# Expert weights in unbroken halves: four neighbouring rows to a partition, in a two-layer MoE and hybrid-mixer kernel

## The chip, the core and the metric

The kernel runs on one NeuronCore of a Trainium2 chip. Its engines are TensorE (PE, matmuls and transposes), VectorE (DVE), ScalarE (ACT), GpSimd (POOL) and SyncE (SP, which here only issues transfers); 16 DMA engines move data between HBM and the on-chip memory. The metric is the device time of one execution in microseconds (us), the median of several runs.

## The reference

A sequence of 512 tokens with 1024 features goes through two blocks of two layers each. Only the feed-forward part of the first block's two layers is touched by the change: a mixture of 16 experts of width 256, of which each token uses two.

```python
def _moe(h, w_router, router_bias, w_gate, w_up, w_down):
    t = h.reshape(b * s, d)
    scores = jax.nn.sigmoid((t @ w_router).astype(jnp.float32))
...
    combine = jnp.sum(jax.nn.one_hot(idx, N_EXPERTS, dtype=jnp.float32) * gate[..., None], 1)
    hg = jnp.einsum('td,edf->tef', t, w_gate)
    hu = jnp.einsum('td,edf->tef', t, w_up)
    act = jax.nn.silu(hg) * hu * combine[..., None].astype(t.dtype)
    y = jnp.einsum('tef,efd->td', act, w_down)
```

Left out is the choice of the two best experts of the best group of four. `w_gate` and `w_up` are [16, 1024, 256] in a layer, `w_down` is [16, 256, 1024].

Everything is float32. The kernel reaches that precision with three products: each matrix is split into a rounded high part and the remainder, its low part, and high x high, high x low and low x high are added.

## The kernel before

**Stages.** The program is a row of stages, each ended by a barrier of all engines. The change touches two kinds, each of which runs twice, once a layer: `norm_to_hT` where it has a `Router` (normalises, transposes, computes the router's scores, and loads small tables), and right behind it `moe` (the expert stage). In the profile the expert stages run from about 584 to 930 us and from about 1512 to 1860 us.

**Blocks of tokens.** `moe` sorts the 1024 (token, expert) pairs into 23 blocks of 128 rows, each of one expert: blocks 0 to 15 are those of experts 0 to 15, and seven more take what overflows. GpSimd scatters the normalised rows to the HBM tensor `slots_x`. For each block, `x_rows(b)` loads 128 rows of 4 KB from there to `x_block`, a row to a partition. TensorE transposes them with eight instructions in `to_features` (to PSUM), ScalarE scales and shifts each of the eight results with a column of `pk` (`mod_pk`, two tables of 8 columns) into `x_exact`, VectorE splits that into high and low parts (`xT_hi`, `xT_lo`), and TensorE multiplies with the gate and up weights. ScalarE and VectorE form silu(gate) x up (`sg`, `act_t`), TensorE transposes it and multiplies with the down weights, VectorE scales the result (`y_block`), and ScalarE's queue stores it to `slots_y`.

**Units of weights.** A block needs three units of 1 MB: A and B, each with half of the expert's gate matrix and half of its up matrix, and C, its down matrix. `BlockUnits.order` is A0 B0 A1 B1 C0 A2 B2 C1 and so on; the SP queue issues their loads in that order, A and B as two transfers of 512 KB (gate, up), C as one of 1 MB, and x_rows(b + 2) behind each C. There are four raw buffers (two in `raw_sep`, two in `ring`), so a load waits until the unit four places before it has been split. ScalarE makes the high part of each unit (L2152, `split_high`), VectorE the low part of A and C (L2206, `split_low`), GpSimd the low part of B from block 2 on (L2059). The parts live in six places, whose names in the profile are `w_hi`/`w_lo`, `hT_hi`/`hT_lo` and `w_more_hi`/`w_more_lo`.

**Which rows a unit holds.** A matrix has 1024 rows of 1 KB, one to an input feature. Before the change, partition p owns the eight neighbouring rows 8p to 8p + 7 (8 KB). Unit A takes the first four of each partition (`ks = slice(0, 4)`), unit B the last four. So each transfer of 512 KB reads 128 pieces of 4 KB that start 8 KB apart: every second 4 KB of the expert's 1 MB. The features that go with slot k are k, 8 + k, 16 + k and so on, so the transposes in `to_features` read their input in steps of 8 elements (32 bytes), and `pk` is loaded with 8 neighbouring values to a partition. The down matrix of unit C is one unbroken megabyte.

**The lines that the steps below name.** L1136 and L1138 store the modulation columns to HBM and load them back as `mod_pk`; L2023 loads `x_block`; L2038 loads unit C, L2044 the two transfers of A or B; L2094 is the transposes, L2102 and L2105 the gate and up products, L2139 and L2143 the down products; L2159 is `x_exact`, L2152 the high parts, L2206 and L2059 the low parts, L2275 and L2276 the split of `x_exact`, L2301 the low part of the transposed activations (`aT_lo`), L2282 `y_block`.

Of the kernel before, what the change touches and what calls it, by code (L numbers as in the profile page):

```python
# [14 lines left out]
P = 128  # L15
S = 512
NT = S // P
D = 1024
KD = D // P
# [1091 lines left out]
class Router:  # L1111
# [16 lines left out]
    def load(self, sp):  # L1128
        k = self.k
# [5 lines left out]
        sp.dma_start(self.tri[:], k.K["causal"][:, 0, :]).then_inc(self.landed, 16)  # L1135
        sp.dma_start(cols.rearrange("(j p) -> p j", p=P), k.mod[:, 24:40], allow_slow_non_contiguous=True).then_inc(self.pk_landed, 16)  # L1136
        sp.wait_ge(self.pk_landed, 16)
        sp.dma_start(self.pk[:], cols.rearrange("(i p k) -> p i k", i=2, k=KD)).then_inc(self.pk_landed, 16)  # L1138
        sp.wait_ge(self.landed, 96)
        sp.wait_ge(self.pk_landed, 32)  # L1140

    def split(self, dve, link):
        V = self.k.nc.vector
# [820 lines left out]
def moe(k, l, hT, wg, wu, wd, grow, router):  # L1964
# [4 lines left out]
    with ExitStack() as c:  # L1969
# [47 lines left out]
        def _(sp):  # L2017
# [7 lines left out]
            for s, (kind, b) in enumerate(U.order):  # L2025
# [11 lines left out]
                if kind == "C":  # L2037
                    sp.dma_start(dst, wd[e].rearrange("e p f n -> p (e f n)")).then_inc(done, 32)  # L2038
                    if b + 2 < NB and b > 0:
                        x_rows(b + 2)  # L2040
                else:
                    ks = slice(0, 4) if kind == "A" else slice(4, 8)
                    for i, w in enumerate((wg, wu)):
                        sp.dma_start(dst[:, i * D:(i + 1) * D], w[e, :, ks, :].rearrange("e p k n -> p (e k n)")).then_inc(done, 16)  # L2044
                if s == EARLY + 1:
                    x_rows(2)

# [22 lines left out]
        def _(pe):  # L2070
# [17 lines left out]
            def to_features(b):  # L2088
                pe.wait_ge(x_landed[b % 2], 16 * (b // 2) + 16)
                if b >= 1:  # L2090
                    pe.wait_ge(ex_done, b)
                v = xb[:, b % 2, :].rearrange("p (f k) -> p k f", k=KD)
                for q in range(KD):
                    mm = pe.transpose(k.ps[:, 2 + q // 4, (q % 4) * P:(q % 4 + 1) * P], v[:, q, :], k.ident[:])  # L2094
                mm.then_inc(t_done, 1)

            def gate_up(b, kind, first, last):
# [11 lines left out]
            for b in range(NB + 1):  # L2109
                v = b - 1  # L2110
# [206 lines left out]
def first_layer(k, l, last_store):  # L2317
# [4 lines left out]
    with ExitStack() as c:  # L2322
# [31 lines left out]
        with ExitStack() as m:  # L2354
            hT = pair_of(nc, m, "hT", [P, KD, S])
            router = Router(k, m)
            norm_to_hT(k, hT, False, LN_EPS, k.mod[:, 32:40], k.mod[:, 24:32], affine=(A["ln1_g"][l], A["ln1_b"][l]), router=router)
            ex = lambda ap, kp: ap.rearrange("l e (p k) n -> l e p k n", k=kp)[l]
            moe(k, l, hT, ex(A["w_exp_gate"], KD), ex(A["w_exp_up"], KD), ex(A["w_exp_down"], 2), g2, router)
    norm_to_hT(k, None, False, LN_EPS, None, None, affine=(A["ln2_g"][l], A["ln2_b"][l]), store=last_store)  # L2360


# [1234 lines left out]
```

## Time and profile before

| | us |
|---|---|
| median of 3 runs | 3776.25 |
| lowest and highest of them | 3766.58, 3776.66 |
| the profiled execution, its own time | 3776.66 |
| its span (first to last instruction) | 3774.8 |

| engine | busy, us | share of the span |
|---|---|---|
| PE (matmul) | 3225.0 | 85% |
| PEld (weight load) | 2560.7 | 68% |
| DVE | 2407.0 | 64% |
| ACT | 1278.6 | 34% |
| POOL | 573.7 | 15% |

The two expert stages are about 345 us each, 18% of the span. These shares are means over stages with different limits; in the expert stages the engines and the transfers stand otherwise than in the rest, so what counts is read from stretches inside them. The profiled execution took 0.41 us more than the median, and its span is 1.9 us under its own time.

### The profile page before, as it was taken

Reading aid. Unit: us, or ns where it says so; the run is one execution under the profiler, and the core shown is the slowest. Engines: PE = TensorE matmul, PEld = TensorE weight load, DVE = VectorE, ACT = ScalarE, POOL = GpSimd, SP = SyncE. Lnnn points to the kernel's source line nnn. Section 1 sums busy time; section 2 is a strip of 40 time slices with the busy share of each in tenths; the row PEclk is TensorE's granted clock in tenths of the full one; section 3 lists DMA queues with packets and bytes.
Section 4 is the critical chain, followed back from the end, with each engine's and each line's share of the span. In section 5 each row is a group of like instructions: output and inputs, shape, how many; then the busy total and the mean of one; then the engine's idle time right before and its main releaser. Section 6 shows DMA issues by size and latency. Waiting matters only on the chain. (4 is left out here: it accounts for less than half of the span.)

```text
span 3774.8 us, 41000 instructions
## 1 busy us (share of the span) xinstructions
PE 3225.0 (85%) x14702; PEld 2560.7 (68%) x14702; DVE 2407.0 (64%) x3790; ACT 1278.6 (34%) x2024; POOL 573.7 (15%) x147
## 2 busy tenths in 40 slices
PE   4999977885699996788489799678999899889999
PEld 4767756664576685666367578566887688667887
DVE  6756676987676657699743746467775564565445
ACT  2323224674323323476322624232111322231111
POOL 0000002443000000234200000102444100004443
PEclk9999988998799998899789799788999899869999
DMA  7643525997554452799552033012443253102232
GB/s 276 221 165 115 193 96 203 338 341 243 196 175 162 149 171 83 260 339 336 212 188 99 9 110 120 27 56 92 142 144 112 86 176 110 73 23 90 89 100 78
DMA packets 290090, 584.97 MB, mean 155 GB/s; under 512 B 26233, under 2 KB 134193, under 8 KB 282732
## 3 DMA queue, kind: packets, MB, share of 16 engines
q1 hardware_dynamic: 277528, 538.91, 42.6%
q10 hardware_dynamic: 7764, 26.85, 1.8%
q0 software_dynamic: 4608, 16.78, 1.2%
q8 instruction: 108, 1.77, 0.2%
q14 instruction: 82, 0.67, 0.1%
HBM read 529.45 MB, written 79.76 MB: 161 GB/s over the span
## 5 line engine op out<-in xcount | busy, mean ns | idle before, releaser
L132 ACT CAST w_hi<-ring 128x2048 fp32r<-128x2048 f32 (+2 forms) x166 | 308.0, 1859 | 1205.6 <-PE ps L282 1032.1
L282 PE MATMUL ps<-hT_hi,w_hi 128*128 128x512 f32 (+1 forms) x1256 | 500.5, 399 | 22.7 <-DVEq L1108 9.2
L282 PE MATMUL ps<-hT_lo,w_hi 128*128 128x512 f32 (+1 forms) x1256 | 498.5, 397 | 0.0
L139 POOL TENSOR_TENSOR w_lo<-ring,w_hi 128x2048 fp32r<-128x2048 f32 x64 | 307.0, 4798 | 1035.1 <-ACTq L2763 649.6
L144 DVE TENSOR_TENSOR w_lo<-ring,w_hi 128x2048 fp32r<-128x2048 f32 (+3 forms) x112 | 245.4, 2195 | 238.4 <-ACT w_hi L132 238.1
L282 PE MATMUL ps<-hT_hi,w_lo 128*128 128x512 f32 (+1 forms) x1256 | 305.3, 395 | 8.4 <-DVE w_lo L144 8.4
L282 PEld LDWEIGHTS ps<-hT_hi,w_hi 128*128 128x128 f32 (+1 forms) x1256 | 238.5, 190 | 83.1 <-DVEq L1108 10.8
L282 PEld LDWEIGHTS ps<-hT_hi,w_lo 128*128 128x128 f32 (+1 forms) x1256 | 235.9, 188 | 65.4 <-DVE w_lo L144 10.1
L1047 DVE SCALAR_TENSOR_TENSOR piece_sums<-pieces,cond,piece_sums 128x512 f32<-128x512 f32 x294 | 220.8, 751 | 87.6 <-DMA pieces<-in_w_ada_dram 54.8
L282 PEld LDWEIGHTS ps<-hT_lo,w_hi 128*128 128x128 f32 (+1 forms) x1256 | 238.5, 190 | 55.6
L282 PE MATMUL ps<-w_hi,hT_hi 128*128 128x512 f32 (+1 forms) x672 | 260.0, 389 | 1.0 <-ACT w_hi L132 1.0
L282 PE MATMUL ps<-w_hi,hT_lo 128*128 128x512 f32 (+1 forms) x672 | 259.0, 387 | 0.0
L1322 PE MATMUL ps<-ident_sb,ring 128*128 128x128 f32 x160 | 37.9, 425 | 205.0 <-ACT ring L1285 150.0
L2053 POOL DMA_INDIRECT slots_x<-ring,rows_r x16 | 26.5, 1656 | 1207.3 <-DVE rows_r L2250 1203.1
L2159 ACT ACTIVATE x_exact<-ps,mod_pk 128x128 f32<-128x128 f32 x368 | 133.7, 468 | 161.1 <-PE ps L2094 161.1
L1322 PEld LDWEIGHTS ps<-ident_sb,ring 128*128 128x128 f32 x160 | 32.6, 229 | 210.0 <-ACT ring L1285 154.2
L282 PE MATMUL ps<-w_hi,hid_hi 128*128 128x512 f32 x448 | 174.4, 389 | 0.0
L282 PE MATMUL ps<-w_hi,hid_lo 128*128 128x512 f32 x448 | 174.4, 389 | 0.0
L2828 DVE TENSOR_TENSOR hid_exact<-hid_exact 128x512 f32<-128x512 f32 x64 | 162.0, 2531 | 4.0 <-DVE hid_exact L2825 0.6
L102 PE MATMUL ps<-ident_sb 128*128 128x128 f32 x796 | 115.4, 317 | 54.1 <-PEq L72 45.5
L282 PE MATMUL ps<-w_lo,hT_hi 128*128 128x512 f32 (+1 forms) x672 | 158.2, 387 | 0.0
L102 PEld LDWEIGHTS ps<-ident_sb 128*128 128x128 f32 x796 | 113.0, 232 | 57.8 <-issue 49.1
(588 smaller groups left out, 6760.5 us busy)
## 6 DMA issues: line engine op xcount, KB each, us to landing
ring<-in_mlp_w_dram SPq DMA_DIRECT2D x64, 1024.0 KB, 5.2
pieces<-in_w_ada_dram SPq DMA_DIRECT2D x96, 512.0 KB, 5.9
ring<-in_w_in_dram SPq DMA_DIRECT2D x36, 1024.0 KB, 6.9
pieces<-in_mod_w_dram SPq DMA_DIRECT2D x72, 512.0 KB, 5.0
raw_sep<-in_w_exp_gate_dram SPq DMA_DIRECT2D x50, 512.0 KB
raw_sep<-in_w_exp_up_dram SPq DMA_DIRECT2D x50, 512.0 KB
raw_sep<-in_w_exp_down_dram SPq DMA_DIRECT2D x24, 1024.0 KB
ring<-in_e_w_in_dram SPq DMA_DIRECT2D x24, 1024.0 KB, 5.5
```

The source lines that it names most:

```text
L102: pe.matmul(k.ps[:, bank, 0:P], k.ident[:], k.ident[:], start=True, stop=True)
L132: self.k.nc.scalar.copy(self.k.parts[0][:, i, 0:words], self.k.ring[:, i, 0:words]).then_inc(self.high, 1)
L139: self.k.nc.gpsimd.tensor_tensor(self.k.parts[1][:, i, 0:words], self.k.ring[:, i, 0:words], self.k.parts[0][:, i, 0:words].bitcast(F32), ...
L144: self.k.nc.vector.tensor_tensor(self.k.parts[1][:, i, 0:words], self.k.ring[:, i, 0:words], self.k.parts[0][:, i, 0:words].bitcast(F32), ...
L282: mm = pe.matmul(out, a if weight_left else b, b if weight_left else a, start=first and part == 0 and q == ks[0] and o == 0, stop=last and ...
L1047: ins = V.scalar_tensor_tensor(acc, slot[:, q, :], f, acc, ALU.mult, ALU.add)
L1322: mm = pe.transpose(k.ps[:, q, t * P:(t + 1) * P], xn[:, t, q * P:(q + 1) * P], k.ident[:])
L2053: nc.gpsimd.indirect_dma_start(k.slots_x, bass.IndirectOffsetOnAxis(rows[:, i, t:t + 1], 0), xn[:, t, :], None).then_inc(scattered, 16)
L2159: last = nc.scalar.activation(ex[:, q, :], k.ps[:, 2 + q // 4, (q % 4) * P:(q % 4 + 1) * P], ACT.Identity, scale=pk[:, 1, q:q + 1], bias=p ...
L2828: link(V.tensor_tensor(e, e, e, ALU.mult))
```

## The change

Unit A now holds the first 512 rows of the gate and of the up matrix, unit B the last 512. Within a half, partition p owns the four neighbouring rows 4p to 4p + 3. So each transfer of 512 KB reads one unbroken stretch of HBM, in pieces of 4 KB that start 4 KB apart, one to a partition. Number, size and order of the transfers stay as they are, and so do their destinations.

Two other places follow from it. The transposes read half of a row at a time in steps of 4 elements (16 bytes), still eight of them, with the same 128x128 results at the same places. And `mod_pk` is loaded in two transfers, one for each half, of four values (16 bytes) to a partition and table, where it was one with eight values (32 bytes); SP then waits for 48 on that semaphore, not 32.

```diff
@@ -1135,9 +1135,10 @@
-        sp.dma_start(self.pk[:], cols.rearrange("(i p k) -> p i k", i=2, k=KD)).then_inc(self.pk_landed, 16)
+        for h in range(2):
+            sp.dma_start(self.pk[:, :, 4 * h:4 * h + 4], cols.rearrange("(i h p k) -> h p i k", i=2, h=2, k=4)[h]).then_inc(self.pk_landed, 16)
         sp.wait_ge(self.landed, 96)
-        sp.wait_ge(self.pk_landed, 32)
+        sp.wait_ge(self.pk_landed, 48)
@@ -2039,9 +2040,9 @@
-                    ks = slice(0, 4) if kind == "A" else slice(4, 8)
+                    h = 0 if kind == "A" else 1
                     for i, w in enumerate((wg, wu)):
-                        sp.dma_start(dst[:, i * D:(i + 1) * D], w[e, :, ks, :].rearrange("e p k n -> p (e k n)")).then_inc(done, 16)
+                        sp.dma_start(dst[:, i * D:(i + 1) * D], w[e, h].rearrange("e p k n -> p (e k n)")).then_inc(done, 16)
@@ -2089,9 +2090,9 @@
-                v = xb[:, b % 2, :].rearrange("p (f k) -> p k f", k=KD)
                 for q in range(KD):
-                    mm = pe.transpose(k.ps[:, 2 + q // 4, (q % 4) * P:(q % 4 + 1) * P], v[:, q, :], k.ident[:])
+                    half = xb[:, b % 2, 512 * (q // 4):512 * (q // 4 + 1)].rearrange("p (f k) -> p k f", k=4)
+                    mm = pe.transpose(k.ps[:, 2 + q // 4, (q % 4) * P:(q % 4 + 1) * P], half[:, q % 4, :], k.ident[:])
@@ -2355,8 +2356,9 @@
-            ex = lambda ap, kp: ap.rearrange("l e (p k) n -> l e p k n", k=kp)[l]
-            moe(k, l, hT, ex(A["w_exp_gate"], KD), ex(A["w_exp_up"], KD), ex(A["w_exp_down"], 2), g2, router)
+            halves = lambda ap: ap.rearrange("l e (h p k) n -> l e h p k n", h=2, k=4)[l]
+            down = A["w_exp_down"].rearrange("l e (p k) n -> l e p k n", k=2)[l]
+            moe(k, l, hT, halves(A["w_exp_gate"]), halves(A["w_exp_up"]), down, g2, router)
```

No instruction changes its place on PE, ACT, DVE or POOL. On SP, at the end of the `norm_to_hT` stage ahead of each expert stage, the instructions stood so before (`scratch` is in HBM, `raw_sep` the raw buffer of the first unit):

```order
L1135 DMA tri_sb<-const_causal_dram 128x128
L1136 DMA scratch<-mod 128x16x1
L1138 DMA mod_pk<-scratch 128x2x8
L68 UNCONDITIONAL_BRANCH
L2016 UNCONDITIONAL_BRANCH
L2044 ISA
L2044 DMA raw_sep<-in_w_exp_gate_dram 128x1024
L2044 DMA raw_sep<-in_w_exp_up_dram 128x1024
```

And they stand so in the changed kernel:

```order
L1135 DMA tri_sb<-const_causal_dram 128x128
L1136 DMA scratch<-mod 128x16x1
L1139 DMA mod_pk<-scratch 128x2x4 x2
L68 UNCONDITIONAL_BRANCH
L2017 UNCONDITIONAL_BRANCH
L2045 ISA
L2045 DMA raw_sep<-in_w_exp_gate_dram 128x1024
L2045 DMA raw_sep<-in_w_exp_up_dram 128x1024
```

One transfer has become two; the branches that follow are the stage's barrier, and the loads of the first expert's unit A come right behind it, with the same shape on the chip's side.

## Rows read from the trace of the kernel before

**Rows 1.** Windows: us, busy of each engine, granted clock, DMA share, GB/s.

```profile
660.00:900.00 240.00, 200.69 (x889) 158.11 (x890) 215.01 (x134) 169.03 (x248) 100.26 (x20) 0.95 0.95 335
1590.00:1830.00 240.00, 201.13 (x889) 158.62 (x889) 215.52 (x134) 168.72 (x247) 98.73 (x20) 0.95 0.95 332
```

**Rows 2.** ACT's waits on transfers: 660 to 900 us, then 1590 to 1830 us.

```profile
ACT w_hi L2152 <- DMA raw_sep<-in_w_exp_down_dram: 1.9, 2, 1.3
ACT w_more_hi L2152 <- DMA ring<-in_w_exp_down_dram: 1.0, 1, 1.0
ACT w_more_hi L2152 <- DMA raw_sep<-in_w_exp_down_dram: 0.7, 1, 0.7
...
ACT w_more_hi L2152 <- DMA raw_sep<-in_w_exp_down_dram: 1.3, 2, 0.9
ACT w_hi L2152 <- DMA raw_sep<-in_w_exp_down_dram: 0.4, 1, 0.4
```

**Rows 3.** Waits of SP's queue and of DVE, 660 to 900 us: total, times, longest.

```profile
SPq L2044 <- DVE w_more_lo L2206: 44.6, 14, 4.9
SPq L2038 <- POOL hT_lo L2059: 33.5, 10, 3.4
...
DVE w_lo L2206 <- ACT w_hi L2152: 10.0, 10, 1.9
```

**Rows 4.** Timeline of DVE and ACT in one block: start, us, instruction, idle before.

```profile
711.31 5.10 DVE L2206 TENSOR_TENSOR w_more_lo<-ring,w_more_hi 128x2048 fp32r<-128x2048 f32 x1 [1.18 <-ACT w_more_hi L2152]
721.86 0.42 DVE L2301 TENSOR_TENSOR aT_lo<-ps,aT_hi 128x256 fp32r<-128x256 f32 x1
722.79 5.78 DVE L2206 TENSOR_TENSOR w_lo<-raw_sep,w_hi 128x2048 fp32r<-128x2048 f32 x1 [0.52 <-ACT w_hi L2152]
...
719.01 3.75 ACT L2152 CAST w_hi<-raw_sep 128x2048 fp32r<-128x2048 f32 x2
```

**Rows 5.** Timeline: DVE's low part of unit C in every third block.

```profile
685.47 5.76 DVE L2206 TENSOR_TENSOR w_more_lo<-raw_sep,w_more_hi 128x2048 fp32r<-128x2048 f32 x1 [0.51 <-ACT w_more_hi L2152]
...
760.07 5.80 DVE L2206 TENSOR_TENSOR w_more_lo<-ring,w_more_hi 128x2048 fp32r<-128x2048 f32 x1 [0.47 <-ACT w_more_hi L2152]
...
797.45 5.72 DVE L2206 TENSOR_TENSOR w_lo<-ring,w_hi 128x2048 fp32r<-128x2048 f32 x1 [0.54 <-ACT w_hi L2152]
...
834.82 5.62 DVE L2206 TENSOR_TENSOR w_more_lo<-raw_sep,w_more_hi 128x2048 fp32r<-128x2048 f32 x1 [0.62 <-ACT w_more_hi L2152]
...
872.64 4.97 DVE L2206 TENSOR_TENSOR w_lo<-raw_sep,w_hi 128x2048 fp32r<-128x2048 f32 x1 [1.27 <-ACT w_hi L2152]
```

**Rows 6.** Timeline: ACT's high parts that waited for a load of unit C.

```profile
771.70 1.90 ACT L2152 CAST w_hi<-raw_sep 128x2048 fp32r<-128x2048 f32 x1 [1.27 <-DMA raw_sep<-in_w_exp_down_dram]
...
858.87 1.91 ACT L2152 CAST w_more_hi<-ring 128x2048 fp32r<-128x2048 f32 x1 [0.97 <-DMA ring<-in_w_exp_down_dram]
...
870.71 1.90 ACT L2152 CAST w_hi<-raw_sep 128x2048 fp32r<-128x2048 f32 x1 [0.64 <-DMA raw_sep<-in_w_exp_down_dram]
```

**Rows 7.** Windows while units A0 and then B0 arrive: columns as in Rows 1.

```profile
588.00:590.00 2.00, 0.00 (x0) 0.00 (x0) 1.83 (x6) 0.00 (x0) 0.00 (x0) 0.55 1.00 307
590.00:592.00 2.00, 0.00 (x0) 0.00 (x0) 1.73 (x9) 1.47 (x1) 0.00 (x0) 0.50 1.01 410
```

**Rows 8.** Timeline: last early low part, and transposes from steps of one and eight.

```profile
620.88 2.29 DVE L2206 TENSOR_TENSOR w_more_lo<-raw_sep,w_more_hi 128x2048 fp32r<-128x2048 f32 x1 [4.28 <-ACT w_more_hi L2152]
...
561.91 1.97 PE L1322 MATMUL ps<-ident_sb,ring 128*128 128x128 f32 x8 [24.65 <-ACT ring L1285]
...
627.35 1.98 PE L2094 MATMUL ps<-ident_sb,x_block 128*128 128x128 f32 x8 [4.78 <-DMA x_block<-slots_x]
```

**Rows 9.** Timeline of SP around the load of mod_pk, and that load's landing times.

```profile
563.62 0.37 SPq L1138 DMA_DIRECT2D mod_pk<-scratch  x1
584.64 0.36 SPq L2044 DMA_DIRECT2D raw_sep<-in_w_exp_gate_dram  x1
...
DMA to landing us min/median/max: 2.1/2.1/2.2
```

## The prediction

> **What bounds the kernel now.** The change works inside the two expert stages, so I read those first, in windows of 240 us from their steady middle [rows 1]. Two things look full there. The 16 DMA engines are busy 0.95 of the time, at 335 and 332 GB/s. DVE is busy 215.01 and 215.52 us of 240, 90%; PE has 84%, ACT 70%. The DMA share alone would say that the stage waits for its weights, and then a better layout in HBM would pay at once. So the second view asks who waits for a landing. In the first window ACT, which takes each unit from its raw buffer, waits for a transfer four times, 1.9 + 1.0 + 0.7 = 3.6 us; in the second three times, 1.3 + 0.4 = 1.7 us [rows 2]. All seven are loads of unit C, the down matrix, whose form the change doesn't touch; not one is a load of A or B. The third view is SP's own waits: its queue stands for tens of microseconds until DVE or POOL has split the unit whose buffer is wanted, 44.6 and 33.5 us in the two largest groups [rows 3]. So buffers, not bytes, set when loads start, and a high DMA share is the sign of loads that arrive just in time.
>
> Who sets the pace, then? The timeline of a block shows a loop of DVE and ACT [rows 4]. DVE's low part of C takes 5.10 to 5.78 us; DVE works on until `aT_lo`, ends that at 722.28, and starts the next C part at 722.79, when ACT's two high parts, which ran back to back from 719.01 to 722.76, are done. The idle time of 0.52 us there is ACT's work, not a transfer: two casts in one unbroken piece show that the second had its data. DVE's waits of this kind come to 10.0 us in ten of the window's blocks [rows 3], nearly all with no transfer behind them.
>
> The starts of DVE's C part repeat in rounds of three blocks, which gives a clean measure of what a late load costs [rows 4, 5]. From 685.47 to 722.79 is 37.32 us, a round in which ACT waits for no load. The rounds to 760.07, 797.45 and 834.82 take 37.28, 37.38 and 37.37; the first of these holds ACT's wait of 0.7 us [rows 2], the second that of 1.27 us at 771.70 [rows 6]. The last, to 872.64, takes 37.82 and holds two waits, 0.97 and 0.64 us. So of 3.6 us of waits about 0.5 us reached the pace; the rest vanished in slack that the round has anyway. A block takes 37.32 / 3 = 12.44 us.
>
> **The change part by part.**
>
> *Loads of A and B.* Same bytes, same count, same pieces of 4 KB; only the distance of the pieces in HBM goes from 8 KB to 4 KB. The most that faster loads can return where they are seen is the waits on C, which queue behind A and B: 3.6 + 1.7 = 5.3 us; by the rounds above it is 0.5 us in the first stage and less in the second, whose waits are smaller. I take 0.5 us in all, and keep 0 to 5.3 for the range.
>
> *The loads at the start of the stage.* Here DMA engines are idle ahead of the loads, and windows show the two halves arriving at different speed: 307 GB/s while A0 comes in, 410 when B0 does, at the same share of 1.0 [rows 7]. Both read every second 4 KB, so the distance of the pieces by itself doesn't forbid 410. A0 could come sooner, 1 MB at 410 and not at 307 being 2.6 and not 3.4 us, 0.9 us less. But nobody needs it: what gates the first block is its rows, scattered by POOL and loaded again. DVE has split the last of the early units at 620.88 + 2.29 = 623.17, and PE starts the first transposes at 627.35, on the landing of `x_block` [rows 8]. Gain 0, with 4.2 us of cover; if that cover were gone, 0.9 us a stage would be seen.
>
> *The transposes.* Eight to a block before and after. Their input steps go from 8 elements to 4. The trace has no step of 4, but it has both sides of it at the same clock of 1.2 GHz: eight transposes with a step of 1 took 1.97 us, eight with a step of 8 took 1.98 us [rows 8]. A step of 4 lies between, so 0, bounded by 0.01 us in either direction, 46 x 0.01 = 0.5 us.
>
> *The load of mod_pk.* SP issues one more transfer, 0.37 us, of shorter pieces. The old one is issued at 563.62 and lands 2.1 us later, at 565.7; the expert stage's first load goes out at 584.64 [rows 9], so SP sits at the barrier for some 18 us. Even if the pair took twice the issue and twice the landing, (0.37 + 2.1) x 2 = 4.9 us, it would be in by 568.6. Nothing stands behind it on SP but that barrier. Cost 0; without the cover 2.5 us a layer, 5 in all. Its only reader, `x_exact`, comes behind the transposes of 627.35 [rows 8].
>
> Sum: -0.5 + 0 + 0 + 0 = -0.5 us, against the profiled execution's own 3776.66: 3776.2. That execution stood 0.4 above the median, so the median becomes 3775.8 us. This is no change: about 0.3%, 11.3 us, is what a measurement of this kernel can tell from none. The three runs shown spread by 10 us by themselves.
>
> **The rivals.**
>
> *The loads were the limit after all (faster).* For it: the share of 0.95, and loads of C that land so close to their use that seven were late. If the stage is paced by bytes, what counts is how fast A and B move. A block moves 12.44 us x 335 GB/s = 4.17 MB, and 2.10 MB of it are A and B. At 335 / 0.95 = 353 GB/s they occupy the engines for 5.94 us; at the 410 that B0 reached [rows 7], for 5.11. That is 0.83 us a block, times 20 full blocks a stage and two stages 33 us: 3743. Against it: the waits of rows 2, the rounds of rows 5, and that DVE alone is 90% busy: even with no wait at all, DVE's 215 us in 240 put a floor of 11.1 us under a block.
> The trace doesn't say why A0 came slower than B0 from the same stretch of HBM. The Trainium skill has a rule that bears on this (DMA: Bandwidth & Descriptors, section Latency and other measured facts): transfers whose rows lie large powers of two apart in HBM run at a fraction of the full rate, and the cure is a pad of some KiB or tiles laid out unbroken. By that rule A and B gain; but its measured distances begin at 512 KiB, ours is 8 KiB, and rows 7 show a load with ours at 410 GB/s. No run here yet shows the unbroken form.
>
> *The loads get faster, or don't, and nobody sees it.* If the slowness of A0 is a cost of the first touch of a stretch of HBM, then B found it paid; now B is a fresh stretch of its own and A touches half as much. The sum over A and B stays, and so does the time. This is the case in which the change doesn't do what its form suggests; it ends at 3775.8 as well and is counted with the forecast.
>
> *Unbroken loads are slower (slower).* One mechanism: the 128 pieces of a transfer now fall into one stretch of 512 KB and not into 1 MB, and if neighbouring pieces get in each other's way, A and B run at less than 353 GB/s. DMA engines have 5% of 12.44 us, 0.6 us a block, free. At the 307 of A0 in both, 2.10 MB take 6.84 us, 0.90 more than 5.94; at least 0.3 a block no longer fits, and C is late in every block: 40 x 0.3 = 12 us, 3788. It decides from 321 GB/s (5.94 + 0.6 us) downwards. Against it: loads of `x_block` have exactly this form, 128 pieces of 4 KB side by side, and in the steady stretch ACT's waits on transfers name none of them [rows 2].
>
> **How the numbers follow.** Forecast, with the second rival in it: 0.79, 3775.8. Loads were the limit: 0.12, 3743, or part of the way there. Unbroken loads slower: 0.09, 3788 and up. The forecast's own range is 3776.2 - 5.3 and 5 us up, widened by the 10 us that runs spread, 3762 to 3787; with 3788 as the slower case's first point it ends at 3788, and only the faster case lies outside. Faster by over 0.3%: 0.13; within: 0.78; slower: 0.09.
>
> **What would show it.** Right: DVE busy about 215 us in 240, rounds of three blocks at 37.3 us, ACT's waits on transfers still a few us and on C alone, or none; L2095's eight transposes at 1.97 us on the slow clock; `mod_pk` landed before 569. A changed DMA share with the same rounds would mean that loads changed and nobody cared. Wrong: rounds well under 37.3 with the DMA share as before would say that bytes set the pace; casts of A or B waiting on transfers, or C late in each block, would be the slower rival. The whole forecast falls if a wait that the profile puts down to ACT's work was in truth a load that landed in the same moment.

## The result: 0.2% slower, and the time went where the change does nothing

The changed kernel took 3776.09 us, median of 20 runs (3771.19 to 3790.16), the kernel before, beside it, 3769.93 (20 runs, 3763.14 to 3785.49). The ratio of the two is 1.002, with a 95% interval of 1.0011 to 1.003. So the time lies inside the predicted range and inside "no change" as the prediction defined it, but the difference has a sign: slower by 4 to 11 us, where the sum said half a microsecond faster.

I go through the rows that the prediction named. First the windows from the steady middle of both expert stages of the changed kernel, with the columns of [rows 1]:

```profile
660.00:900.00 240.00, 200.04 (x883) 158.22 (x881) 218.85 (x136) 169.95 (x250) 97.21 (x19) 0.95 0.95 338
1590.00:1830.00 240.00, 200.60 (x887) 159.07 (x887) 217.28 (x137) 170.72 (x251) 96.63 (x19) 0.95 0.94 337
```

The DMA share and the GB/s are those of before. VectorE reads 2 to 4 us more, which is the position of the window against the blocks (136 and 137 instructions where there were 134), not slower work: its split of C still takes 5.1 to 5.7 us, once 6.0. Next the waits in the two windows (engine, tile and line, releaser: us in total, times, longest), which answer [rows 2] and [rows 3]:

```profile
ACT x_exact L2160 <- PE ps L2095: 70.1, 19, 5.2
DVE w_lo L2207 <- ACT w_hi L2153: 7.1, 9, 1.2
DVE w_more_lo L2207 <- ACT w_more_hi L2153: 7.1, 10, 1.2
...
ACT w_more_hi L2153 <- DMA ring<-in_w_exp_down_dram: 0.9, 1, 0.9
```

The last row is the second window's only wait of ACT for a transfer; the first window has none. Before they came to 3.6 and 1.7 us. So fewer loads come late, and it buys nothing. The transposes of the first block and the load of `mod_pk`, as in [rows 8] and [rows 9]:

```profile
631.60 1.98 PE L2095 MATMUL ps<-ident_sb,x_block 128*128 128x128 f32 x8 [4.77 <-DMA x_block<-slots_x]
...
566.09 0.89 SPq L1139 DMA_DIRECT2D mod_pk<-scratch  x2
588.57 0.36 SPq L2045 DMA_DIRECT2D raw_sep<-in_w_exp_gate_dram  x1
```

As forecast, 1.98 us at 1.2 GHz, and SP has some 22 us between the pair and the first load. The second transfer doesn't lengthen the stage either: from the start of SP's `mod_pk` load to the expert stage's first load it was 21.02 us before [rows 9] and is 22.48 here, but 21.06 in another profile of the same kernel (`after_third` below).

Where, then, are the 6 us? I lined up all 14702 matmuls of the two profiles. The offsets change in many places by a few microseconds at a time, and most of these differ as much between two profiles of one kernel. (The largest such spread in all 20 profiles of this document is in one stage that begins near 2390 us: 108 to 125 us, with the change or without.) One place does not. It lies 2700 us behind the first changed instruction and 1400 us behind the last, in the second block, where sliding-window attention follows retention. These are windows that follow that stage from its start, first of the kernel before, then of the changed one; the columns are those of [rows 1], so the third number from the right is the clock that TensorE was granted (1.00 is 2.4 GHz, 0.50 is 1.2 GHz):

```profile
3278.38:3298.38 20.00, 19.31 (x93) 14.32 (x93) 13.66 (x77) 9.53 (x34) 0.00 (x0) 0.84 0.62 238
3298.38:3338.38 40.00, 40.00 (x131) 28.37 (x130) 28.27 (x144) 13.66 (x55) 0.00 (x0) 0.50 0.00 1
3338.38:3358.38 20.00, 17.48 (x62) 11.59 (x61) 14.32 (x45) 8.12 (x15) 0.00 (x0) 0.63 0.00 1
3358.38:3388.38 30.00, 29.99 (x111) 20.99 (x110) 15.49 (x17) 10.20 (x18) 0.00 (x0) 0.89 0.22 70
3388.38:3428.38 40.00, 27.81 (x101) 19.84 (x102) 25.48 (x27) 12.65 (x15) 11.60 (x3) 0.79 0.17 53
3428.38:3449.52 21.14, 21.14 (x92) 17.03 (x91) 15.89 (x16) 3.83 (x2) 8.83 (x3) 1.00 0.27 99
```

```profile
3282.51:3302.51 20.00, 19.53 (x87) 14.35 (x88) 13.04 (x72) 8.79 (x31) 0.00 (x0) 0.76 0.63 238
3302.51:3342.51 40.00, 40.00 (x130) 28.33 (x131) 28.38 (x146) 13.72 (x54) 0.00 (x0) 0.50 0.00 1
3342.51:3362.51 20.00, 17.47 (x62) 12.79 (x63) 13.47 (x48) 8.80 (x18) 0.00 (x0) 0.54 0.00 1
3362.51:3392.51 30.00, 30.00 (x91) 18.48 (x90) 11.77 (x12) 6.53 (x11) 0.00 (x0) 0.77 0.22 70
3392.51:3432.51 40.00, 28.85 (x96) 18.72 (x95) 26.57 (x26) 14.41 (x21) 9.16 (x2) 0.70 0.09 28
3432.51:3460.93 28.42, 28.42 (x123) 22.90 (x122) 20.24 (x21) 5.74 (x3) 11.29 (x3) 1.00 0.33 109
```

Both end at the same VectorE instruction, L2828 before and L2830 after, which takes 4.4 us. Before, the way there is 171.14 us, after 178.42: 7.28 us more for the same work. The stretch crosses two more barriers, so it is not one stage: the attention stage itself takes 1.6 us more, the stage behind it 5.7. For short, the whole stretch is called the attention stage below. What a window has at the lower clock is twice what is missing to 1.00: before 6.4 + 40 + 14.8 + 6.6 + 16.8 + 0 = 85 us, after 9.6 + 40 + 18.4 + 13.8 + 24 + 0 = 106 us.

### The profile page after: what moved, and what is told of

Same layout as the page of the kernel before. It is cut to its first block and busy times, and to the rows that moved or that the text cites. A ratio compares the mean times of both kernels' runs of the same rounds, so it can differ in the third digit from the quotient of the medians.

```text
span 3786.2 us, 41002 instructions
## 1 busy us (share of the span) xinstructions
PE 3233.6 (85%) x14702; PEld 2569.0 (68%) x14702; DVE 2410.2 (64%) x3790; ACT 1277.3 (34%) x2024; POOL 569.7 (15%) x147
## 5 line engine op out<-in xcount | busy, mean ns | idle before, releaser
L2830 DVE TENSOR_TENSOR hid_exact<-hid_exact 128x512 f32<-128x512 f32 x64 | 162.0, 2532 | 4.0 <-DVE hid_exact L2827 0.6
```

The costliest lines, as they stand in the source:

```text
L2830: link(V.tensor_tensor(e, e, e, ALU.mult))
```

## The experiments

Each kernel ran 12 times (`shift_a` 11, `c_half` once), beside runs of the kernel before on the same chip. Where an expectation counts "units of 3.4 us", it counts the low-clock time of this stretch: 25 units are the 85 us above, 31 are the 106.

### The change in parts

`loads_only` is the kernel before with A and B loaded as unbroken halves, and `pk_only` the kernel before with `mod_pk` in two transfers (the values as before):

```diff
-                    ks = slice(0, 4) if kind == "A" else slice(4, 8)
+                    h = 0 if kind == "A" else 1
...
+                        sp.dma_start(dst[:, i * D:(i + 1) * D], w[e, h].rearrange("e p k n -> p (e k n)")).then_inc(done, 16)
```

```diff
+        for h in range(2):
+            sp.dma_start(self.pk[:, :, 4 * h:4 * h + 4], cols.rearrange("(i p h k) -> h p i k", i=2, h=2, k=4)[h]).then_inc(self.pk_landed, 16)
```

> Units A and B hold unbroken halves as in the change, but the transposes and mod_pk stay as they were, so each feature meets the wrong row of the gate and up matrices (the products are not those of the reference). Theory 1: as pk_only and before_again within 0.001. Theory 2: 1.002, the whole of what the change costs, with the expert stages 3 us longer each.

> The kernel before with mod_pk loaded in two transfers of four columns each, the same values. Theory 1: within 0.001 of before_again in the ratio, the stage before each expert stage not longer (24.16 us from the first rstd of the second normalisation to the first instruction of the expert stage on ACT). A third theory, that the second transfer holds SP at the stage's end: some 1 to 3 us in each of these two stages.

> The changed kernel once more. Theory 1: ratio between 1.000 and 1.003, expert stages within 1.5 us of those of before (341.9 and 342.4 us in its first profile), the rest of any difference outside them, where low-clock stretches sit elsewhere. Theory 2: 1.002, with both expert stages some 3 us longer than in the profile of the kernel before that is taken beside it.

> The kernel before against itself, as the measure of what a comparison of no change gives. Theory 1 (the 0.2% comes from TensorE's stretches at the lower granted clock, which fall differently from run to run and from kernel to kernel): ratio 1.000 within 0.002, the two expert stages, from their first weight load to the first row written back, within 1 us of 340.9 and 342.2 us, and any difference of the span outside them beside another total of low-clock time. Theory 2 (the unbroken loads cost something in the expert stage): the same here, since nothing is changed.

Measured, as ratios to the kernel before: `loads_only` 1.0006 (0.9988 to 1.0024), `pk_only` 1.0017 (1.0000 to 1.0035), the changed kernel again 1.0017 (1.0001 to 1.0033), the kernel before again 1.0003 (0.9987 to 1.0018). So the least suspected edit, a hidden load of 8 KB cut in two, is the one with a number, at the edge of its interval.

`loads_only` also answers what the layout does to a load. Windows of 1 us while unit A0 arrives, first `pk_only` (every second 4 KB), then `loads_only` (unbroken):

```profile
588.57:589.57 1.00, 0.22 (x4) 0.12 (x2) 0.68 (x3) 0.00 (x0) 0.00 (x0) 1.00 1.03 287
589.57:590.57 1.00, 0.00 (x0) 0.00 (x0) 0.93 (x3) 0.00 (x0) 0.00 (x0) 0.53 1.05 315
590.57:591.57 1.00, 0.00 (x0) 0.00 (x0) 0.93 (x3) 0.00 (x0) 0.00 (x0) 0.50 0.89 332
```

```profile
587.88:588.88 1.00, 0.40 (x4) 0.29 (x3) 0.49 (x3) 0.00 (x0) 0.00 (x0) 0.50 1.01 410
588.88:589.88 1.00, 0.00 (x0) 0.00 (x0) 0.93 (x3) 0.00 (x0) 0.00 (x0) 0.50 1.04 410
589.88:590.88 1.00, 0.00 (x0) 0.00 (x0) 0.93 (x3) 0.00 (x0) 0.00 (x0) 0.50 1.03 422
```

The unbroken unit comes at 410 to 422 GB/s, the spaced one at 287 to 332. The same holds in all 20 profiles, at the start of both expert stages, in windows of 1 us from 2 to 5 us behind the first issue: the twelve kernels with spaced loads have 229 to 344 GB/s there, the eight with unbroken loads 381 to 438, but for three windows of 48 (307, 348 and 365).

### Transposes, the split again, and shifts of start times

`tr_only` takes the new transposes alone; `pk_again` is `pk_only` once more. The two shifts, VectorE writing 128x512 or 128x1536 zeros at the end of each expert stage, test whether any small delay would do the same, by moving what TensorE's low clock falls on. The diff is that of `shift_a`:

```diff
                     link(V.scalar_tensor_tensor(k.x[:, t, :], src, wts[:, i, t:t + 1], k.x[:, t, :], ALU.mult, ALU.add))
+            link(V.memset(yb[:].rearrange("p b n -> p (b n)")[:, 0:512], 0.0))
```

> The kernel before with the transposes alone changed: they read each half of a row in steps of 4 elements; loads of the weights and of mod_pk are as before. Its output is not the reference's, since the weights still come with steps of 8; amount and order of the work are the same. In the profile of the changed kernel the eight transposes of a block take 1.11 us at the high clock where before they took 1.05. Theory 1 (the transposes' 0.06 us reach the pace in part): L2093 takes 1.11 us at the high clock, and aT_lo of block 15 stands about 0.2 to 0.3 us later against that of block 0 than before in both expert stages, as in both profiles of the changed kernel (0.25 and 0.34; 0.24 and 0.28), with the loads of before; 46 x 0.06 = 2.8 us is the most it can cost, 0.7 us what the rounds show. Rival (the loads made the rounds longer): 1.11 us, but rounds as before. If the transposes carry the whole +6 us of the change, the median is about 3776; if 0.7 us, about 3771.

> The kernel with only the load of mod_pk split in two, timed once more (its first 12 timings stood 5 us above the kernel before, with an uncertainty of as much). Theory 1 (the split does nothing, the first result was scatter): the median is within 2 us of the kernel before. Theory 2 (this edit carries most of the change's +6 us, by way of how long TensorE stands at its low clock): again about +5 us, a mean granted clock lower by .002, and in the profile again a longer low-clock part at 3290 to 3460 us, where its first profile lost 6.9 us against the kernel before.

> The kernel before with one useless instruction: at the end of each expert stage VectorE writes zeros over 128x512 of y_block, which nobody reads again. All that follows starts some 0.55 us later each time, 1.1 us in all; nothing else changes. Theory 1 (where the low-clock stretches fall depends on when the work starts, to tenths of a microsecond, and decides several us): the median moves by anything from -5 to +7 us, not by 1.1, and the mean granted clock moves with it, by about .0004 for each us. Theory 2 (the clock follows the amount of work only, and the changed kernel's +6 us is work of its own): +1.1 us, 3771 to 3772, clock as before.

> As the first shift, with 128x1536 elements: 1.6 us each time, 3.3 us in all. Theory 1 (start times decide how the low-clock stretches fall): a median that departs from +3.3 us by some us in either direction, by another amount than in the first shift, with the mean granted clock to match. Theory 2: +3.3 us, about 3774, clock as before.

Measured: `tr_only` 0.9997 (0.9986 to 1.0008), `pk_again` 1.0015 (1.0004 to 1.0025), `shift_a` 1.0001 (0.9990 to 1.0011), `shift_b` 1.0011 (1.0001 to 1.0022). The delays cost no more than they last, within the intervals (1.1 and 3.3 us are 1.0003 and 1.0009). My theory 1, that any shift of the start times redraws the low clock by several us, fell: both profiles show the attention stage exactly as before, 171.1 us. The split of `mod_pk` cost again.

`tr_only` settled the transposes. Eight of them at 2.4 GHz, from the timeline of TensorE, in `before` and in `tr_only`:

```profile
713.11 1.04 PE L2094 MATMUL ps<-ident_sb,x_block 128*128 128x128 f32 x8
725.20 1.05 PE L2094 MATMUL ps<-ident_sb,x_block 128*128 128x128 f32 x8
```

```profile
718.75 1.11 PE L2094 MATMUL ps<-ident_sb,x_block 128*128 128x128 f32 x8
730.84 1.11 PE L2094 MATMUL ps<-ident_sb,x_block 128*128 128x128 f32 x8
```

A step of 4 costs 0.06 us more than one of 8, at the full clock only. It reaches the pace in part. The start of `aT_lo` in four blocks in a row gives one round, in `loads_only` (transposes of before) and in `tr_only`:

```profile
711.59 0.42 DVE L2301 TENSOR_TENSOR aT_lo<-ps,aT_hi 128x256 fp32r<-128x256 f32 x1
...
723.72 0.42 DVE L2301 TENSOR_TENSOR aT_lo<-ps,aT_hi 128x256 fp32r<-128x256 f32 x1
...
735.86 0.42 DVE L2301 TENSOR_TENSOR aT_lo<-ps,aT_hi 128x256 fp32r<-128x256 f32 x1
...
748.90 0.41 DVE L2301 TENSOR_TENSOR aT_lo<-ps,aT_hi 128x256 fp32r<-128x256 f32 x1
```

```profile
715.36 0.42 DVE L2301 TENSOR_TENSOR aT_lo<-ps,aT_hi 128x256 fp32r<-128x256 f32 x1
...
727.49 0.42 DVE L2301 TENSOR_TENSOR aT_lo<-ps,aT_hi 128x256 fp32r<-128x256 f32 x1
...
739.63 0.42 DVE L2301 TENSOR_TENSOR aT_lo<-ps,aT_hi 128x256 fp32r<-128x256 f32 x1
...
752.72 0.42 DVE L2301 TENSOR_TENSOR aT_lo<-ps,aT_hi 128x256 fp32r<-128x256 f32 x1
```

37.31 us against 37.36; the rounds that follow take 37.30 and 37.35. The median round of both expert stages is 37.36 to 37.38 us in the eight profiles with the new transposes and 37.29 to 37.32 in the twelve with the old ones, whichever way the weights come. So 0.06 us of three times 0.06 is seen, 0.02 us a block, times 40 full blocks 0.8 us.

The single blocks say where: 12.13, 12.14 and 13.04 us in `loads_only`, 12.13, 12.14 and 13.09 in `tr_only`. All of it is in the third, long block. A short and a long block of `before` differ in the granted clock, the third number from the right (columns as in [rows 1]):

```profile
759.20:771.30 12.10, 9.89 (x46) 7.73 (x46) 11.59 (x8) 7.90 (x13) 5.32 (x2) 1.00 0.96 350
771.30:784.40 13.10, 11.29 (x46) 8.95 (x46) 10.33 (x9) 9.24 (x14) 4.72 (x2) 0.87 0.96 348
```

At full clock VectorE is busy 11.59 us of a block of 12.1, and slower transposes don't show. Where the granted clock is 0.87, the block takes 0.9 us more and holds TensorE's 0.06 us too.

### What differs at the attention stage

The ten profiles up to here show what the four with the split have in common. It lies one stage ahead, at a stage switch. VectorE's timeline there, in `before` and in the changed kernel (the bracket is the idle time before the instruction):

```profile
3210.79 0.42 DVE L3276 COPY y_ret<-ps 128x256 f32<-128x256 f32 x1
...
3212.61 0.06 DVE L731 MEMSET eps_h<- 128x1 f32 x1 [1.40 <-PEq L859]
```

```profile
3215.25 0.43 DVE L3278 COPY y_ret<-ps 128x256 f32<-128x256 f32 x1
3216.75 0.06 DVE L731 MEMSET eps_h<- 128x1 f32 x1 [1.08 <-PEq L859]
```

The switch takes 1.40 us before and 1.08 after, so all engines start that stage 0.32 us sooner, and the attention stage behind it too. That is an odd way to lose 7 us, so I put three claims to the test: that any extra instruction of SP does it (`tri_split`, where `tri_sb`, another table that SP loads ahead of the expert stage, comes in two transfers), that giving the 0.33 us back removes the loss (`after_delay`, `pk_delay`), and, apart from that, that bytes don't pace the expert stage (`c_half`).

```diff
+        for h in range(2):
+            sp.dma_start(self.tri[:, 64 * h:64 * h + 64], k.K["causal"][:, 0, 64 * h:64 * h + 64]).then_inc(self.landed, 16)
```

```diff
                 dve.wait_ge(y_done, 2 * NT)
+                if H.after is not None:
+                    nc.vector.memset(H.sq[:, 1, 0:160], 0.0).then_inc(y_done, 1)
+                    dve.wait_ge(y_done, 2 * NT + 1)
```

```diff
+                    sp.dma_start(dst[:, 0:D], wd[e, :, 0:1, :].rearrange("e p f n -> p (e f n)")).then_inc(done, 32)
```

> The kernel before, where SP loads not mod_pk but another small table of the same stage, tri_sb, in two transfers of 64 columns instead of one of 128. So SP has one instruction more at nearly the same place; pieces of mod_pk and everything else are as before. In all six profiles so far without the second mod_pk transfer, VectorE stands 1.40 us at the start of the stage of L731 near 3200 to 3213 us (after the loops of the stage before it), in all four with it 1.07 or 1.08, and with that the whole stage starts 0.33 us earlier; three of these four then show TensorE for 31 units of 3.4 us and not 25 at the low clock up to 3460 us, 6.9 us lost by the stage that follows. Theory A (it is the extra instruction, not what it loads): that wait is 1.07 us here too, the same longer low clock, and the median is about 5 us above the kernel before. Theory B (the short pieces of mod_pk do it): 1.40 us and the time of before.

> The changed kernel with one useless instruction: in the stage that starts at about 3217 us, VectorE at its end writes zeros over 128x160 of a dead buffer, which makes everything after it 0.33 us later; this puts back the 0.33 us by which that stage starts earlier than in the kernel before. Theory A (the changed kernel is slower mostly because the next stage, at 3280 us, begins 0.3 us too early for the clock): the delay makes it faster, about 5 us under the changed kernel, to within 2 us of the kernel before, and the low clock from 3280 to 3460 us goes back from 31 units of 3.4 us to 25. Rival (that stage's longer low clock is chance): 0.3 us slower than the changed kernel, 5 to 7 us above before.

> The kernel with mod_pk in two transfers, and the same 0.33 us of useless work in the stage that starts at about 3200 us. Theory A: the +5 us of the split are gone, the median is within 2 us of the kernel before, 25 units of low clock at 3280 to 3460 us where both profiles of the split alone have 31. Rival (the split costs by another way): still about +5 us.

> The kernel before, with unit C's load halved: only the first of its two rows of 4 KB to a partition is read, so every block moves 2.6 MB and not 3.1 MB; casts, splits and products work on the full buffer as before, so its output is not the reference's. Theory of the prediction (buffers and engines pace the expert stage, not bytes): rounds of three blocks stay at 37.3 us or fall by 0.1 us at most, the DMA share falls from 0.95 to about 0.80, ACT's waits on transfers are gone, and the time stays within 3 us of before. Rival (bytes pace it): rounds shorten towards 37.3 x 5/6 = 31 us, stopped by VectorE at about 33.5; the time falls by up to 50 us.

Measured: `tri_split` 1.0020 (1.0005 to 1.0035), with the wait at 1.08 us and 178.4 us to the 4.4-us instruction. So what is loaded doesn't matter. `pk_delay` 1.0003 (0.9988 to 1.0017) and `after_delay` 1.0015 (0.9998 to 1.0031); in both profiles the wait is 1.07, the delay stands behind it, and the attention stage is back at 171.1 us. The profiles say that the stretch's loss is gone. The first median fits that; the second, 5 us above before and uncertain by as much, is not the 2 us that the expectation wanted.

`c_half` moves a sixth less. Its first window:

```profile
660.00:900.00 240.00, 198.89 (x880) 156.40 (x879) 219.29 (x136) 171.20 (x250) 98.02 (x20) 0.95 0.88 294
```

Rounds of `aT_lo` are 37.30, 37.31 and 37.30 us, as before. ACT's waits on transfers, 3.6 and 1.7 us before, are down to one of 0.2 us. The share fell to 0.88 only, not to 0.80 as I had expected, with 294 GB/s for 335. This may come from how I halved the load: the number of packets in the run stayed 290090, with 288620 of them under 8 KB where there were 282732, so C comes in as many packets of half the size. The kernel was timed once, at 3770.27 us, beside a median of 3766.16 for the kernel before; it is the rounds that say that bytes don't pace this stage.

### The change without its extra instruction

The four pieces of `mod_pk` that the new layout needs fit in one transfer:

```diff
-        for h in range(2):
-            sp.dma_start(self.pk[:, :, 4 * h:4 * h + 4], cols.rearrange("(i h p k) -> h p i k", i=2, h=2, k=4)[h]).then_inc(self.pk_landed, 16)
+        sp.dma_start(self.pk[:].rearrange("p i (h k) -> p (i h) k", h=2), cols.rearrange("(j p k) -> p j k", j=4, k=4)).then_inc(self.pk_landed, 16)
```

> The changed kernel with mod_pk loaded in one transfer: 4 pieces of 16 bytes to a partition, the same 16-byte pieces as in the changed kernel, the same values at the same places, but one instruction of SP less, as many as before the change. Theory A (the extra SP instruction costs 5 to 7 us by way of the clock; loads and transposes 1 to 2 us): VectorE's wait at the start of the stage of L732 is 1.40 us again, 25 to 28 units of 3.4 us at the low clock from 3280 to 3460 us and not 31, and the median is 1 to 3 us above the kernel before, 4 us or more under the changed kernel. Theory B (16-byte pieces of mod_pk, or loads and transposes, cost the 6 us): about as slow as the changed kernel.

> The same kernel once more, for an interval half as wide: theory A 1 to 3 us above before, theory B 5 us or more.

> The changed kernel itself, beside the others on one chip: 5 to 8 us above the kernel before by both theories, wait of 1.07 us, 27 to 31 units of low clock.

> The changed kernel with 0.33 us of useless work in the stage at about 3217 us, timed once more (the first 12 timings stood 5.0 us above before, uncertain by 4.7). Theory A: 2 to 3 us above before (loads and transposes, and the delay itself), 3 us or more under the changed kernel. Rival (loads or transposes cost 5 us of their own): 5 us above before.

Measured on one chip: `after_one` 1.0004 (0.9991 to 1.0016) and its repeat `after_one_2` 1.0009 (0.9997 to 1.0022); `after_third` 1.0020 (1.0007 to 1.0033); `after_delay_2` 0.9996 (0.9982 to 1.0010). With the layout complete and the instruction gone, the wait is 1.40 again, the attention stage 171.1 us, and most of the loss is gone. The repeat with the delay shows no loss, below the 2 to 3 us that was expected; the three measurements with the delay (1.0003, 1.0015, 0.9996) are 1.0005 in the mean.

Last, where the instruction stands and how many there are. `late_split` loads `mod_sums` in two transfers, in the attention stage itself, so behind the switch; `two_splits` splits both `mod_pk` and `tri_sb`.

> The kernel before, where SP loads mod_sums in two transfers instead of one, in the stage near 3280 us, so behind the stage switch whose length changed. Theory A (what counts is an instruction of SP that stands ahead of that switch): VectorE's wait at L731 stays 1.40 us, the low clock from 3280 to 3452 us stays at 25 units of 3.4 us, the stage up to L2828 takes 171.1 us as before, and the time is within 3 us of the kernel before. Rival (any added SP instruction costs this): 1.07 us and 5 us slower.

> The kernel before with both mod_pk and tri_sb loaded in two transfers: two more SP instructions at the place where one was enough for 5.5 us. Theory A1 (more instructions ahead, shorter switch each time): the wait at L731 is 0.7 to 0.8 us, the low clock of the next stage falls in yet another way, and the time is not to be told. Theory A2 (the switch has only the two lengths, 1.40 and 1.07): 1.07 again with 31 units and +5 us, or 1.40 again with 25 units and the time of before.

Measured: `late_split` 0.9996 (0.9982 to 1.0010), wait 1.40, 171.2 us. `two_splits` 1.0025 (1.0005 to 1.0045), wait 1.08, 178.5 us. Behind the switch it costs nothing, and the switch has only the two lengths here.

### What the switch does

The page's table of DMA queues has a row for q14, kind "instruction", 82 transfers of 8 KB in the run. Transfers in windows around the switch, in `before` from 3211.2 to 3212.8 us (queue, kind: packets, MB, share of 16 engines):

```profile
q14 instruction: 1, 0.01, 2.1%
```

In `tri_split` the window of the switch, 3200.9 to 3202.2 us, is empty, and the transfer is found 22 us earlier, from 3178 to 3180 us, inside the loops of retention:

```profile
DMA packets 0, 0.00 MB, mean 0 GB/s; under 512 B 0, under 2 KB 0, under 8 KB 0
```

```profile
q1 hardware_dynamic: 411, 0.81, 104.1%
q14 instruction: 1, 0.01, 1.0%
```

The neighbours in the row of q14 (some 47 us before the switch, 66.8 behind it) are in the same places in both. Against the count of matmuls this is the only one of the 82 that moves, by about 100 matmuls; the others stay within 30 of their place in all 20 profiles, but for one in `two_splits` that moves by 51. (Each split stands twice in the program, once a layer, so SP has two instructions more, and four in `two_splits`; `late_split` adds only one.)

What the shorter switch is made of stands in the rows of its barrier, L72, where each engine arrives with a DRAIN instruction and none goes on before the last has come. First `before`, then `tri_split` (engine, instruction, its length in ns three times over, its start):

```profile
L72 PEldq DRAIN  x1: 13/13/13, 3211.8 to 3211.8; - x1
L72 SPq DRAIN  x1: 124/124/124, 3212.0 to 3212.0; - x1
```

```profile
L72 SPq DRAIN  x1: 7/7/7, 3201.4 to 3201.4; - x1
...
L72 PEldq DRAIN  x1: 13/13/13, 3201.5 to 3201.5; - x1
```

In the ten profiles with the long switch SP comes to this barrier last, 0.22 us behind PE, and stays in its drain for 124 ns; in the ten others it comes 0.07 us ahead of PE and takes 7 ns. So it is SP itself that holds the long switch up, as the engine whose program was changed. The 20 profiles together:

| profiles | one or two SP transfers more in the stage ahead of each expert stage | q14 transfer at the switch | wait at L731 | start of attention stage to the 4.4-us instruction |
|---|---|---|---|---|
| before (2), shift_a, shift_b, loads_only, late_split, after_one (2) | no | yes | 1.40 | 171.1 to 171.2 |
| tr_only, c_half | no | yes | 1.40 | 174.9, 172.5 |
| after (2 of 3), pk_only, pk_again, tri_split, two_splits | yes | no | 1.07, 1.08 | 178.4 to 178.5 |
| after_again | yes | no | 1.07 | 172.9 |
| after_delay (2), pk_delay | yes, and 0.33 us of delay | no | 1.07 | 171.1 |

The middle columns know no exception in 20. The last has three: `tr_only`, `c_half` and `after_again`.

Then the clock. Windows from the attention stage's first 17 us, at the same distances from its start, in `before` and after:

```profile
3281.88:3291.78 9.90, 9.44 (x52) 6.53 (x50) 7.72 (x45) 5.00 (x20) 0.00 (x0) 1.00 1.02 407
3291.98:3294.78 2.80, 2.58 (x13) 1.50 (x13) 2.56 (x16) 1.33 (x6) 0.00 (x0) 1.00 0.05 19
```

```profile
3286.01:3295.91 9.90, 9.44 (x52) 6.55 (x51) 7.61 (x44) 4.86 (x20) 0.00 (x0) 1.00 1.02 403
3296.11:3298.91 2.80, 2.80 (x11) 1.92 (x10) 2.59 (x15) 1.33 (x7) 0.00 (x0) 0.50 0.05 22
```

TensorE has done the same up to the second row, 9.44 us busy of 9.90 at 2.4 GHz. Then the changed kernel falls to 1.2 GHz sooner and, by the windows of the first section, comes back later and falls for longer in the products that follow.

The record of the granted clock shows what the 0.3 us move. TensorE idles for 3.5 us ahead of the attention stage, and in that time the clock falls to 1.2 GHz: 0.48 us before the stage's first matmul in `before`, 0.16 us before it in the changed kernel. The long low part begins 16.6 us behind that matmul in the one and 13.5 us behind it in the other. In all 20 profiles, the clock falls 0.42 to 0.52 us ahead in the eight of the table's first row, in the three with the delay and in `tr_only`; 0.13 to 0.18 us ahead in the six of the third row; and 0.79 and 1.33 us behind the first matmul in `c_half` and `after_again`. So two of the three exceptions have the fall in another place, and `tr_only` alone stays unexplained. That the start decides it, the three profiles with the delay bear out; why the chip then grants the clock so, no run shows. The Trainium skill (CRC Debugging, section Comparing the Two Runs) calls queue 14 that of the sequencer's instruction refills. By that, and since SP's program alone got longer, one instruction more moves the place where a piece of SP's program ends, and the refill falls into the loops ahead. The trace agrees in the transfer's place, ten profiles against ten. That the refill is what delays SP is not shown: the record of its transfer begins 0.1 us behind the new stage's first instruction (0.35 in `loads_only`), when SP's delay is over.

## Why the prediction was right in its parts and wrong in its sum

- **The number was luck.** 3775.8 us was forecast and 3776.09 measured, but the forecast started from a median of three runs, 3776.25, which stood 6.3 us above the 3769.93 of twenty, and the change then cost what the base had too much. The range doesn't follow from its own terms either: 3776.2 less 5.3 and plus 5, widened by 10, is 3761 to 3791, not 3762 to 3787.
- **What bounds the stage: right, with a gap.** Steady rounds stayed within 0.1 us of 37.3, ACT's waits on transfers fell from 5.3 to 0.9 us without effect, and `c_half` took away a sixth of the bytes at no gain. The rival of 3743 us is out. The loop of DVE and ACT sets 12.13 us a block, though, not the mean of 12.44: the rest is the third block, 0.9 us longer at a granted clock of 0.87.
- **Loads of A and B, −0.5 us: too small to be seen, and its derivation was wrong.** Ratios of `loads_only` and `after_one` (1.0004 to 1.0009) exclude a gain of 5 us. The 0.5 us came from one round of DVE's C part, 37.82 us with two waits in it; the starts of `aT_lo` in that stretch of `before` (846.68 and 884.00) are 37.32 us apart, and in `c_half`, almost without such waits, the rounds are the same. So the waits gave the pace nothing, and the term is 0. The rival in which the slowness of A0 is a cost of the first touch is wrong as a mechanism: A0 came at 410 GB/s when unbroken, so the layout did matter there. That nobody sees it is right. "Unbroken loads slower" is wrong.
- **Transposes, 0 bounded by 0.01 us: wrong, and small.** The step was to compare steps of 1 and 8 and to place 4 between. I took both rows at 1.2 GHz, where all three steps take 1.97 to 1.99 us. At 2.4 GHz a step of 4 takes 1.11 and one of 8 1.04 or 1.05. An interpolation was no bound. Priced rightly it is 0.06 us, 0.02 of it on the pace, 0.8 us in all.
- **The load of `mod_pk`, "Cost 0": this is the step that failed.** The working looked at when SP issues, when it lands and who waits, and all of that held: SP still stands for some 20 us between the landing and the first load of the expert stage. It missed that the transfer is also an instruction in SP's program, which changed a stage switch 1700 us later. The four measurements of the kernel before with one or two transfers more and no delay (`pk_only`, `pk_again`, `tri_split`, `two_splits`) came to 1.0017, 1.0015, 1.0020 and 1.0025, the seven others without one ahead of the switch (leaving out `shift_b`, a delay by itself) to 0.9996 to 1.0009. The mean difference is about 0.17%, 6.4 us, and the stage switch with the attention stage accounts for 7.28 - 0.32 = 6.96 us wherever the profile shows the long form. The changed kernel itself came to 1.002, 1.0017 and 1.0020, so the split accounts for all that it lost, as far as these intervals can tell.
- **The sum** went from the changed stages only and took the rest of the program as fixed, adding the spread between runs to the range. A sum over stages holds if no other stage changes by itself; here the switch and the stretch behind it did. The direct part, loads and transposes together, is 1.0004 and 1.0009 in 24 runs, 1.5 to 3.4 us with an uncertainty of as much: it agrees with the +0.3 us that −0.5 and +0.8 make, and with 3.

What stays open: whether the refill is what delays SP at the switch, why the clock's grant hangs on 0.3 us, why the clock's fall stands elsewhere in `c_half` and `after_again`, and why `tr_only` has 174.9 us with the fall in its usual place.

## What to carry to other kernels

When a small edit moves the time and its own stage hasn't moved, line the two profiles up instruction by instruction and look for the first stage that differs in every pair; then move the suspected cause alone (the same instruction elsewhere, the same delay without the instruction) before believing it. Keep the number of instructions on a queue as it was when only a layout changes: here the same layout with one transfer of four pieces, `after_one`, avoids most of the loss. And price a transposed or strided read at the clock at which it mostly runs, at its own step, since at 1.2 GHz it may look free.

## What the runs showed of the hardware that I had not expected

- An instruction added to SP's queue in each of two stages moved an 8-KB instruction load from a stage switch into a loop 22 us earlier and shortened the switch from 1.40 to 1.07 us, 1700 us behind the last time that the added instruction ran; that saving of 0.33 us led to 7.28 us more in the stretch that follows.
- At the long switch SP came to the barrier last, 0.22 us behind TensorE, in ten profiles of ten.
- Transposes that read SBUF in steps of 16 bytes (4 elements) took 1.11 us for eight at 2.4 GHz, in steps of 32 bytes 1.05; at 1.2 GHz some 1.98 both.
- A load of 128 pieces of 4 KB ran at 381 to 438 GB/s at the start of an expert stage when the pieces touch in HBM (three windows of 48 lower), and at 229 to 344 with 4 KB between them, though spaced loads reached 410 a few us later [rows 7].
- Halving one of three loads of 1 MB took the DMA engines' busy share from 0.95 to 0.88 while GB/s fell from 335 to 294, with the number of packets as before: the share doesn't follow the bytes.
